# Layer norms of whole 1,024-column tiles over a four-bank accumulator tensor, with mean and variance inside ScalarE's square and root

## The reference, cut to what matters

```python
LN_EPS = 1e-5
DN_ALPHA = (2 * DEPTH) ** 0.25          # DEPTH = 2

def layer_norm(x, g, b):
    xf = x.astype(jnp.float32)
    mu = xf.mean(-1, keepdims=True)
    var = jnp.square(xf - mu).mean(-1, keepdims=True)
    return ((xf - mu) * lax.rsqrt(var + LN_EPS) * g + b).astype(x.dtype)

for layer in range(DEPTH):
    mix = mixer_ab(...) or mixer_c(...)
    h = layer_norm(DN_ALPHA * h + mix, ln_g[layer, 0], ln_b[layer, 0])
    ffn = peer(h, ...)
    h = layer_norm(DN_ALPHA * h + ffn, ln_g[layer, 1], ln_b[layer, 1])
```

## Time and profile before

| | |
|---|---|
| median of three runs | 2946.8 us (2946.26 to 2952.04) |
| profiled execution, span | 2948.8 us |
| PE (TensorE matmul) busy | 2881.0 us, 98% |
| DVE (VectorE) busy | 2038.9 us, 69% |
| ACT (ScalarE) busy | 1572.4 us, 53% |
| POOL (GpSimd) busy | 920.7 us, 31% |
| mean granted clock of TensorE | 0.988 of full speed |
| share of TensorE in the chain that ended last | 89% |

### The profile page before, as it was taken

One profiled execution on the slowest core, in us unless ns is written; L12 is line 12 of the kernel. 1 busy time (PEld: TensorE's weight loads), 2 busy tenths in 40 slices (PEclk: granted clock), 3 DMA queues, 4 the chain that ended last, 5 costly groups with the idle time before them and its releaser, 6 DMA issues.

```text
span 2948.8 us, 63115 instructions
## 1 busy us (share of the span) xinstructions
PE 2881.0 (98%) x21369; PEld 2620.5 (89%) x21369; DVE 2038.9 (69%) x4326; ACT 1572.4 (53%) x2603; POOL 920.7 (31%) x369
## 2 busy tenths in 40 slices
PE   8999999999999989999999999899999999999999
PEld 7899999888888879999998888788799999988887
DVE  4379578888555645947788865675629767788755
ACT  3444444677555544444457755553644544477654
POOL 3689600000004757980000000155779820000000
PEclk9999999999999989999999999999999999999999
DMA  6455555555664435555555566444555555555565
GB/s 209 150 173 183 180 170 171 172 172 177 221 193 155 145 119 169 184 183 167 170 172 172 176 218 193 149 130 122 158 178 179 185 176 167 171 174 174 186 193 163
DMA packets 142991, 508.63 MB, mean 172 GB/s; under 512 B 17169, under 2 KB 18193, under 8 KB 142881
## 3 DMA queue, kind: packets, MB, share of 16 engines
q1 hardware_dynamic: 142880, 507.16, 54.0%
HBM read 506.05 MB, written 1.05 MB: 172 GB/s over the span
## 4 chain that ended last, share of the span: by engine, by line
PE 89%; DVE 4%; POOL 2%; ACT 2%; issue 2%; DMA 0%; SPq 0%; DVEq 0%; ACTq 0%; POOLq 0%
PE col L541 15%; PE col L543 15%; PE col L542 15%; PE acc L541 13%; PE acc L543 12%; PE acc L542 12%; POOL w_lo L492 2%; PE acc L674 2%; PE col L674 2%; PE acc L634 1%; DVE work L1911 1%; ACT w_hi L801 1%; ACT work L860 0%; PE acc L615 0%; PE acc L2179 0%
## 5 line engine op out<-in xcount | busy, mean ns | idle before, releaser
L492 POOL TENSOR_TENSOR w_lo<-ring,w_hi 128x1024 fp32r<-128x1024 f32 x365 | 920.5, 2531 | 1457.6 <-ACT w_hi L801 1457.1
L801 ACT ACTIVATE w_hi<-ring 128x1024 fp32r<-128x1024 f32 x941 | 993.8, 1056 | 517.4 <-PE acc L543 425.6
L541 PE MATMUL col<-x_hi,w_hi 128*128 128x256 f32 (+1 forms) x3976 | 1134.1, 285 | 8.1 <-DVE x_lo L1056 4.4
L542 PE MATMUL col<-x_lo,w_hi 128*128 128x256 f32 (+1 forms) x3976 | 1121.4, 282 | 0.0
L543 PE MATMUL col<-x_hi,w_lo 128*128 128x256 f32 (+1 forms) x3976 | 1120.9, 282 | 0.0
L492 DVE TENSOR_TENSOR w_lo<-ring,w_hi 128x1024 fp32r<-128x1024 f32 x576 | 704.1, 1223 | 279.9 <-ACT w_hi L801 279.9
L541 PEld LDWEIGHTS col<-x_hi,w_hi 128*128 128x128 f32 x3976 | 754.3, 190 | 13.1 <-issue 7.7
L543 PEld LDWEIGHTS col<-x_hi,w_lo 128*128 128x128 f32 x3976 | 754.9, 190 | 0.0
L542 PEld LDWEIGHTS col<-x_lo,w_hi 128*128 128x128 f32 x3976 | 752.7, 189 | 0.7
L541 PE MATMUL acc<-w_hi,c_hi 128*128 128x512 f32 x1664 | 659.7, 396 | 5.9 <-DVE c_lo L1210 2.0
L543 PE MATMUL acc<-w_hi,c_lo 128*128 128x512 f32 x1664 | 649.3, 390 | 0.0
(11 more groups left out here) (294 smaller groups left out, 1992.0 us busy)
## 6 DMA issues: line engine op xcount, KB each, us to landing
ring<-in_u SPq DMA_DIRECT2D x384, 512.0 KB, 3.3
ring<-in_v SPq DMA_DIRECT2D x384, 512.0 KB, 3.7
ring<-in_wq SPq DMA_DIRECT2D x48, 512.0 KB, 3.4
ring<-in_s_in SPq DMA_DIRECT2D x21, 512.0 KB, 3.6
ring<-in_c_in SPq DMA_DIRECT2D x16, 512.0 KB, 3.3
ring<-in_s_out SPq DMA_DIRECT2D x16, 512.0 KB, 3.6
ring<-in_s_gate SPq DMA_DIRECT2D x12, 512.0 KB, 3.6
ring<-in_s_conv SPq DMA_DIRECT2D x12, 512.0 KB, 3.6
```

The source lines that it names most:

```text
L492: eng.tensor_tensor(k.w_lo[s.slot][:, :], k.ring[s.slot][:, :], k.w_hi[s.slot][:, :].bitcast(F32), ALU.subtract).then_inc(k.lo[s.slot], 1)
L541: pe.matmul(out, a[0], b[0], start=start, stop=False, **kw)
L542: pe.matmul(out, a[0], b[1], start=False, stop=False, **kw)
L801: act.activation(k.w_hi[s.slot][:, :], k.ring[s.slot][:, :], ACT.Copy).then_inc(k.hi[s.slot], 1)
```

## The change: what it does

The four banks become one tensor `acc_all` of 2,048 columns, `acc[i]` is its i-th bank. In a layer norm:

- The residual is one operation of 1,024 columns per tile. It reads `h` and two banks, writes `h` in SBUF (not PSUM), and its accumulated row sum goes straight to ScalarE (semaphore `mean`).
- ScalarE squares a whole tile from `h`, with scale -D and the row sum as bias, so that it gets (row sum - D x) squared, D squared times the squared deviation. The root then uses scale 1/D^3 and eps as bias. VectorE's variance operation and its wait are gone. ScalarE does square and root of tile 0, splits slab end + 1, and does square and root of tile 1; before "s" it then splits slab end + 2 at once, elsewhere behind the copies to `x_hi`, as before.
- VectorE computes minus the mean itself, then centres a whole tile in one operation: from `h` and the gain to the `NORMED` part of `work` (all in SBUF). The scalings, still in halves, read that part and the bias, and write `h`.
- VectorE's order is: residual 0, centre 0, residual 1, scalings of tile 0, centre 1, scalings of tile 1.

The residuals of the RMS norms keep their operations.

```diff
-        self.acc = [ps(f"acc{i}", [P, 512]) for i in range(4)]
+        self.acc_all = ps("acc", [P, 4 * 512])
+        self.acc = [self.acc_all[:, i * 512:(i + 1) * 512] for i in range(4)]
...
-    def centred_squares(self, t):
-
-        k = self.k
+    def centred_std(self, t):
+
+        k, act = self.k, self.act
         self.w.next(k.mean)
-        for half in range(2):
-            self.square(k.acc[t * 2 + half][:, :], 2 * t + half, bias=k.small[:, 20 + t:21 + t])
+        self.square(k.h[:, t, :], 2 * t, bias=k.small[:, 16 + t:17 + t], scale=-float(D))
+        act.wait_ge(k.sq, self.w.count(k.sq))
+        act.activation(k.small[:, 8 + t:9 + t], k.small[:, 40 + 2 * t:41 + 2 * t], ACT.Sqrt, bias=k.small[:, 49:50],
+                       scale=1.0 / D ** 3).then_inc(k.std, 1)
...
-        eps = k.small[:, 49:50]
+        self.centred_std(0)
+        self.split_lead(Slab(end + 1))
+        self.centred_std(1)
         if after != ("s",):
-            for t in range(NT):
-                self.centred_squares(t)
-            for t in range(NT):
-                self.tile_std(t, eps)
-            self.split_lead(Slab(end + 1))
             self.lead_x([0])
             self.lead_x([1])
             self.split_lead(Slab(end + 2))
         else:
-            for t in range(NT):
-                self.centred_squares(t)
-                if t:
-                    self.tile_std(0, eps)
-                self.split_lead(Slab(end + 1 + t))
-            self.tile_std(1, eps)
+            self.split_lead(Slab(end + 2))
             self.lead_meta()
...
-        def residual(t, half):
-            self.add_residual(t, half, last, DN_ALPHA, sums=True)
-
-        def minus_mean(t):
+        def residual(t):
+            self.w.next(k.tile_full)
+            if t:
+                dve.wait_ge(k.used, last + 1)
+            dve.scalar_tensor_tensor(k.h[:, t, :], k.h[:, t, :], DN_ALPHA, k.acc_all[:, t * D:(t + 1) * D],
+                                     ALU.mult, ALU.add, accum_out=k.small[:, 16 + t:17 + t]).then_inc(k.mean, 1)
+            self.w.skip(k.mean, 1)
+
+        def centre(t):
+            dve.wait_ge(k.mean, means + t + 1)
+            own.do(dve.tensor_scalar(k.small[:, 20 + t:21 + t], k.small[:, 16 + t:17 + t], -1.0 / D, None, ALU.mult))
             own.join()
...
-        def centre(t, half):
...
+            own.do(dve.scalar_tensor_tensor(view(k.big, NORMED + t * D, D), k.h[:, t, :], k.small[:, 20 + t:21 + t],
+                                            gain, ALU.add, ALU.mult))
...
         def scale(t, half):
-            cut, acc = slice(half * 512, (half + 1) * 512), k.acc[t * 2 + half][:, :]
-            dve.scalar_tensor_tensor(k.h[:, t, cut], acc, k.small[:, 12 + t:13 + t], bias[:, cut], ALU.mult, ALU.add)\
-               .then_inc(k.rms_in if rms_next else k.h_part, 1)
...
+            cut = slice(half * 512, (half + 1) * 512)
+            dve.scalar_tensor_tensor(k.h[:, t, cut], view(k.big, NORMED + t * D, D)[:, cut], k.small[:, 12 + t:13 + t],
+                                     bias[:, cut], ALU.mult, ALU.add).then_inc(k.rms_in if rms_next else k.h_part, 1)
+
+        residual(0)
         self.w.next(k.param[slot], 32)
...
+        centre(0)
+        residual(1)
         self.inverse_std(0)
         scale(0, 0)
         scale(0, 1)
+        centre(1)
         self.inverse_std(1)
         scale(1, 0)
+        self.w.skip(k.sq, NT)
```

More of the change, by code:

```diff
@@ L202, in __init__ @@
         self.half_done = sem("half_of_slab_done")
-        self.mean = sem("mean_ready")
+        self.mean = sem("row_sum_ready")
         self.xt = sem("x_transposed")
@@ L843, in std, with tile_std, square @@
         act.activation(dst, src, ACT.Sqrt, bias=bias).then_inc(k.std, 1)
-    def centred_squares(self, t):
-        k = self.k
+    def centred_std(self, t):
+        k, act = self.k, self.act
         self.w.next(k.mean)
-        for half in range(2):
-            self.square(k.acc[t * 2 + half][:, :], 2 * t + half, bias=k.small[:, 20 + t:21 + t])
-    def tile_std(self, t, bias=0.0):
-        self.std(self.k.small[:, 4 + t:5 + t], self.k.small[:, 8 + t:9 + t], bias)
-    def square(self, src, n, bias=0.0):
+        self.square(k.h[:, t, :], 2 * t, bias=k.small[:, 16 + t:17 + t], scale=-float(D))
+        act.wait_ge(k.sq, self.w.count(k.sq))
+        act.activation(k.small[:, 8 + t:9 + t], k.small[:, 40 + 2 * t:41 + 2 * t], ACT.Sqrt, bias=k.small[:, 49:50],
+                       scale=1.0 / D ** 3).then_inc(k.std, 1)
+    def tile_std(self, t):
+        self.std(self.k.small[:, 4 + t:5 + t], self.k.small[:, 8 + t:9 + t])
+    def square(self, src, n, bias=0.0, scale=1.0):
         k, act, rows, cols = self.k, self.act, src.shape[0], src.shape[1]
@@ L859, in square @@
             act.wait_ge(k.sq, self.w.count(k.sq))
-        act.activation(view(k.big, JUNK, cols, p=rows), src, ACT.Square, bias=bias, accum_out=k.small[0:rows, 40 + n:41 + n])\
-           .then_inc(k.sq, 1)
+        act.activation(view(k.big, JUNK, cols, p=rows), src, ACT.Square, bias=bias, scale=scale,
+                       accum_out=k.small[0:rows, 40 + n:41 + n]).then_inc(k.sq, 1)
         self.w.skip(k.sq, 1)
@@ L1060, in rest_x, with add_residual @@
         w.skip(k.xhi, 4)
-    def add_residual(self, t, half, last, alpha, sums=False, saved=False):
-        k, dve, own = self.k, self.dve, self.own
+    def add_residual(self, t, half, last):
+        k, dve = self.k, self.dve
         if half == 0:
@@ L1069, in add_residual @@
         acc, h = k.acc[t * 2 + half][:, :], k.h[:, t, half * 512:(half + 1) * 512]
[L1070 to L1075, removed]
+        dve.scalar_tensor_tensor(h, h, 1.0, acc, ALU.mult, ALU.add).then_inc(k.rms_in, 1)
     def inverse_std(self, t):
@@ L1087, in layer_norm @@
         means = self.w.count(k.mean)
-        def residual(t, half):
-            self.add_residual(t, half, last, DN_ALPHA, sums=True)
-        def minus_mean(t):
-            own.join()
-            dve.tensor_scalar(k.small[:, 20 + t:21 + t], k.small[:, 16 + 2 * t:17 + 2 * t],
-                              k.small[:, 17 + 2 * t:18 + 2 * t], -1.0 / D, ALU.add, ALU.mult).then_inc(k.mean, 1)
-            self.w.skip(k.mean, 1)
-        def centre(t, half):
[L1099 to L1103, removed]
@@ L1105, in variance @@
-        def variance(t):
-            dve.tensor_scalar(k.small[:, 4 + t:5 + t], k.small[:, 40 + 2 * t:41 + 2 * t],
-                              k.small[:, 41 + 2 * t:42 + 2 * t], 1.0 / D, ALU.add, ALU.mult).then_inc(k.var, 1)
-        def scale(t, half):
-            cut, acc = slice(half * 512, (half + 1) * 512), k.acc[t * 2 + half][:, :]
-            dve.scalar_tensor_tensor(k.h[:, t, cut], acc, k.small[:, 12 + t:13 + t], bias[:, cut], ALU.mult, ALU.add)\
-               .then_inc(k.rms_in if rms_next else k.h_part, 1)
@@ L1114, in layer_norm @@
[L1114 to L1117, removed]
-        self.w.next(k.param[slot], 32)
[L1119 to L1127, removed]
+        def residual(t):
[5 more added lines that the diff above has]
+            self.w.skip(k.mean, 1)
@@ L1150, in finish_rms @@
                     self.mean_square(0)
-                self.add_residual(t, half, last, 1.0, saved=True)
+                self.add_residual(t, half, last)
         self.rms_norm(0, slot)
```

## The result

The changed kernel took 2953.2 us (median of 21 runs, 2950.8 to 2957.0) against 2949.1 us for the kernel before on the same chips (21 runs, 2945.7 to 2952.4). The ratio is 1.0016, with a 95% interval of 1.0010 to 1.0022. The forecast was +3.5. The forecast time, 2950.3 us, was built on the median of three runs, 2946.8 us; the longer series puts that base at 2949.1, and this makes 2.3 of the 2.9 us between forecast and measured time. The profiled execution has a span of 2951.3 us, 2.5 us more than that of before.

A forecast was written before the change was run, and what follows sets the result against it. TensorE holds 89% of the chain, so only its standstills, such as the four layer norms, pay. Three norms at +0.32 us and the fourth at +2.56 give +3.5 us on 2946.8: 2950.3 us, range 2941 to 2954.

The forecast's parts named there:

- Residual and read: Norm start: residual over two PSUM banks takes 1.22 us; bounds 0.1 us cheaper, 0.7 us dearer; ScalarE's square starts at 1.32.
- Reciprocal and the first scaling: Tile 0: root done at 2.68, reciprocal at 4.08, first scaling could start at 4.27 us, 2.6 us sooner than before.
- The exclusion: First three norms: GpSimd, 3.80 to 6.17, holds the scalings with two SBUF inputs; first matmul 12.33 us, +0.32 us each.
- The fourth norm: Norm before "s": GpSimd holds both centrings and the scalings; TensorE released at 15.86 us against 13.30, +2.56 us.
- The clock: TensorE's clock still falls to 0.5 in each norm, costing 1.6 us in the next stage's matmuls, as before.
- The sum: Whole kernel: 3 x 0.32 + 2.56 = +3.5 us, put on the median 2946.8 for 2950.3 us.
- rival C: Forecast order, but the clock's return shifts: at most 2 us over four norms, 2948 to 2953; forecast with this scatter 0.63.
- One slip: Layer norms: the prediction said no matmul work hides any of the interval from residual to first matmul, 12.01 us or 15.92.
- A: No exclusion in the norms: first matmul 10.58 us, -5.1 us, 2941.7; 2935 if three norms keep the clock; chance 0.13.
- B: ScalarE's w_hi late, GpSimd asks after the first scaling: +0.9 us in three norms, about +2.6 in the fourth, 2952.1; 0.10.
- D: Fourth norm: GpSimd's third subtraction comes too late to meet VectorE, +0.6 us there, +1.5 us in all, 2948.3; chance 0.14.

The follow-up runs named there:

- a1: Changed kernel, but the centring writes the PSUM accumulator and the scalings read it there: 2946.6 us, ratio 1.0000 to the kernel before.
- a2: Changed kernel, SBUF operand kept, but ScalarE splits the next slabs later, so GpSimd's subtractions come later: 2943.4 us, ratio 0.9983 to the kernel before.
- b1: Kernel before, but in three norms ScalarE splits slab end + 1 between the squares of both tiles, so GpSimd comes early: 2947.8 us, ratio 0.9998.
- a3: Changed kernel with the edits of a1 and a2 together: 2943.2 us, ratio 0.9986 to the kernel before.

## Why the prediction came out right, step by step

**Residual and read.** Forecast 1.22 us, measured 1.22 (1.20 in the fourth norm). So the instruction over two PSUM banks cost neither the 0.1 us less nor the 0.7 us more of the bounds. Its read was done at 1.22 (forecast 1.28), ScalarE's square started at 1.26 (1.32) and the centring at 1.52 (1.56).

**Reciprocal and the first scaling.** It started at 4.13 (forecast 4.27). The root was done at 2.84, not 2.68, since the square took longer than the one of the earlier trace rows, but VectorE's own residual 1 sets this point.

**The exclusion.** GpSimd 3.85 to 6.20 (forecast 3.80 to 6.17), transposes from 6.80 in the third norm (forecast 6.81), centring 1 from 7.51 (7.54), first scaling of tile 1 from 8.90 (8.93). The first scaling itself ended 0.55 us behind GpSimd, where the forecast had 0.60: the pair took 3.27 us, and a second scaling adds 0.66. First matmul 12.33, as forecast. a1, a2 and b1 show this is cause and not coincidence: take the second SBUF operand away or GpSimd away, and the scalings return to 1.41 us. By the Trainium skill, page "SBUF — State Buffer", section "SBUF: two separate sides", it is an exclusive lock held for a whole instruction. The runs agree: the centring in a1 ended 1.09 us behind GpSimd's end, most of a whole operation of 1.28 us, so that little of it can have run beside GpSimd.

**The fourth norm.** The one mis-sized term: +2.21 us instead of +2.56. Centring 0 ended at 3.42 (forecast 3.47), centring 1 at 10.68 (10.83): 0.15 us there, since GpSimd was done at 9.60 (9.69) and the rest of the centring took 1.08 us (1.14). The sums and scaling (1,1) behind it followed 0.21 us closer: RMS scaling of tile 0 from 12.56 instead of 12.92. From there to TensorE it was 2.95 us, as in the earlier trace rows.

**The clock.** It fell in all four norms, and the stage after the third kept its 74.78 us. It fell even behind a much shorter standstill, where I had given it a chance of staying up: in a2 TensorE stood for 2.26 us ahead of the transposes, and the window 1069.90 to 1070.40 shows 0.60:

```profile
1069.90:1070.40 0.50, 0.50 (x4) 0.34 (x3) 0.47 (x3) 0.49 (x2) 0.00 (x0) 0.60 0.00 0
```

**The sum.** 3 x 0.32 + 2.21 = +3.2 us against the measured +4.7 (+2.9 to +6.5). The 1.5 us between them are inside the interval. That the forecast +3.5 lies nearer to +4.7 than these +3.2 is luck: the term of the fourth norm was 0.35 us too large. In the profiled pair the spans differ by less than the norms, +2.5 us: stretch 1, 2 and the last are 0.6, 0.3 and 2.2 us longer in the changed kernel, but its first residual comes at 90.57 instead of 94.30, ahead of any changed operation. For this last the windows from 62.5 to 69.3 give the reason: a granted clock of 0.50 in the kernel before and 1.00 in the changed one, and 6.8 us at half speed cost 3.4 of the 3.7 us. Such shifts come with where the clock's falls land, which is rival C; that they explain the 1.5 us was not shown.

**One slip.** The prediction says that no matmul work hides any of a norm. By its own figures TensorE works on until 2.69 us after the first residual. Nothing follows from it, since both kernels have that stretch.

**The rivals.** A (no exclusion, 10.58 us a norm) fell on the first scaling of 2.6 us. Its arithmetic was nearly right for norms without a hold: 10.35 to 10.47 us in a2; a1, where centring 1 is still held, has 10.85. What it promised of the clock was wrong: it did not stay up with a standstill of 2.3 us. B fell: GpSimd led the scaling by 0.28 us, and 0.84 us in the fourth norm. The 0.28 us was a thin margin. D fell: the third subtraction started at 7.19, and centring 1 met it (3.19 us).

## What to carry to other kernels

Before an operand is moved from PSUM to SBUF, count the SBUF inputs of the VectorE operation and ask what GpSimd does at that moment: here a loss of 4.7 us became a gain of 5.0 when GpSimd came later (a2), and no measurable difference when only the operand went back (a1). When an instruction that releases GpSimd is moved up, that GpSimd work is moved up too, and what it then meets on VectorE is part of the price. Folding small operations into another engine's is worth only what it saves on the chain that ends last, here 0.1 us of 1.5.

## What the hardware showed that was not expected

- The exclusion took in an operation of one column: a sum took 0.96 us instead of 0.15 and ended 0.02 us behind GpSimd (a1, one instance; the kernel before has one of 0.19 us).
- Of a held operation 0.55 us of 0.75 (512 columns) and 1.08 us of 1.28 (1,024 columns) were left after GpSimd's end, 0.20 us less than the whole in both.
- One VectorE instruction over two PSUM banks took 1.22 us for 1,024 columns, no more than its columns ask for by the earlier trace rows.
- Unused matmuls kept the clock at 1.0 through what had been TensorE's standstills of 5.0 and 8.2 us. Each norm gained its 0.4 to 0.7 us, but of four stages behind them only two kept the 1.7 us. In a2 and a3 the clock fell although TensorE stood still for 2.3 us only ahead of the transposes.
